# Value projections of attention and retention packed into three blocks of 256 columns, in a two-stage fp32 network on one core

## The chip, the core and the metric

The kernel runs on one core of one Trainium2 chip, in one launch. The metric is the device time of that core in microseconds (us), taken as the median of several executions. Engines are named as in the profile: PE is TensorE (PEld its weight loads), ACT is ScalarE, DVE is VectorE, POOL is GpSimd, SP is SyncE, which issues the DMAs.

## The reference

The input is one sequence of 512 tokens with 1,024 features. The first stage has two layers; the second stage (feed-forward, state-space scan, dilated attention, cross-attention, feed-forward) is untouched by the change and is left out here. A layer of the first stage is:

```
h = rms_norm(x, g_mix_pre)
u = h @ w_in                                   # 1024 -> 3*384 + 512 + 4*384 = 3200 columns
aq, ak, av, cu, rq, rk, rv, rg = jnp.split(u, SPLITS, axis=-1)
y_att  = chunk_attention(aq, ak, av, rel_bias)  # 6 heads of 64, softmax
y_conv = conv_module(cu, ...)                   # 31 taps, layer norm, silu
y_ret  = retention(rq, rk, rv, rg)              # 6 heads of 64, rotary, decay, layer norm, gate
mix = jnp.concatenate([y_att, y_conv, y_ret], axis=-1) @ w_out
x = x + rms_norm(mix, g_mix_post)
...                                             # then the MLP with w_up, w_down
```

`av` and `rv`, 384 columns each, are the two value projections that the change is about.

## The kernel before, in words

**Products in three parts.** Weights and activations are fp32 and are split into a rounded part (`w_hi`, `h_hi`) and a rest (`w_lo`, `h_lo`). A product is three matmuls per 128-deep slice of the contraction: hi by hi, hi by lo, lo by hi. `product` (line 360) does one block: for each output tile, 8 slices of 3 matmuls.

**Blocks.** The weights are cut into blocks of at most 256 columns (`WCOLS`), in a list made by `layer_pieces` (line 135). A layer has 50 of them. The first 14, which form `w_in`, are in this order (numbered within the layer):

- 0, 1: the convolution's input; 2, 3, 4: attention's queries and keys
- 5 (256 columns), 6 (128 columns): attention's values `av`
- 7, 8, 9: retention's queries and keys `rqk`
- 10 (256), 11 (128): retention's values `rv`
- 12 (256), 13 (128): retention's gate `rg`

Block 14 is the first of `w_out`. A block is of one of two kinds. In a "feat" block the weights are stationary and the 512 tokens stream, so each matmul has 512 columns and the block one tile per 128 output columns. In a "tok" block, which the values are, 128 tokens are stationary and the block's weight columns stream, so each matmul has 256 or 128 columns and there are four tiles, one per 128 tokens: 4 x 8 x 3 = 96 matmuls whether the block is 256 or 128 wide. Two "tok" tiles share a PSUM bank.

**What travels with a block.** Three engines prepare block n+2 while TensorE works: SP loads it into `w_raw` (`load_block`), ACT rounds it (`round_block`, line 339) after its copies of block n out of PSUM, and DVE subtracts to get the rest (`rest_block`, line 350). TensorE waits for that rest before the block. ACT copies each finished tile out of PSUM (`evacuate`, `evacuate_one`).

**The order of the work** is written out by hand for each engine, for one layer at a time; semaphores tie the engines together. From block 8 (`SOFT_AT`) on, attention's softmax is interleaved. It has 24 steps (6 heads by 4 query tiles of 128, the keys growing from 128 to 512 within a head). In step i TensorE (`attend`, line 767) does the scores of i, transposes the probabilities of i-2 (`turn`), and multiplies those of i-3 by the values (`mix`); in steps 8, 10, ... 18 it also does one `swapped` matmul for retention's rotary embedding. DVE (`attend`, line 1192) adds the bias to the scores of i, takes the reciprocal of the sum of i-1, the maximum of i, scales i-1, and in those even steps does three rotary instructions. ACT (`softmax`, line 987) takes the exponential of i and copies the transposed i-2 out of PSUM. The scores and the rotary swaps take turns in a ring of two PSUM banks, so scores wait until DVE has read the one two places before.

Steps are put in "feat" blocks halfway through each tile and behind it, in "tok" blocks only behind each tile: `slots_of` (line 616) gives a "feat" block two steps per tile and a "tok" block one. That makes 4 steps each in blocks 8 to 12 and 2 in block 13, 22 in all; the rest follow among retention's scores. DVE and ACT do the preparation of block n+2 behind the steps of block n.

Beside blocks 1 to 6 DVE computes the convolution's 62 taps, 11 per block; TensorE waits for the last behind block 7 (`MEAN_AT`).

Of the kernel before, what the change touches and what calls it, by code (L numbers as in the profile page):

```python
# [22 lines left out]
P = 128  # L23
# [110 lines left out]

def layer_pieces():

    out = []
    a = ATT_W

    def feat(c0, c1):  # L140
        for c in range(c0, c1, WCOLS):
            out.append(Piece(0, c, min(WCOLS, c1 - c), KD, "feat", "w_in"))

    def tok(c0, c1):
        for c in range(c0, c1, WCOLS):
            out.append(Piece(0, c, min(WCOLS, c1 - c), KD, "tok", "w_in"))


    feat(3 * a, 3 * a + 2 * CONV_W)
    feat(0, 2 * a)  # L150
    tok(2 * a, 3 * a)
    r = 3 * a + 2 * CONV_W
    feat(r, r + 2 * RET_W)
    tok(r + 2 * RET_W, r + 3 * RET_W)
    feat(r + 3 * RET_W, r + 4 * RET_W)
    for c in range(0, DM, WCOLS):
        out.append(Piece(0, c, WCOLS, KD, "feat", "w_out"))
    for half in range(2):
        for j in range(8):
            out.append(Piece(0, half * 2048 + j * WCOLS, WCOLS, KD, "feat", "w_up"))  # L160
        for j in range(4):
            for kb in range(2):
                out.append(Piece(half * 2048 + kb * KB, j * WCOLS, WCOLS, KD, "feat", "w_down",
                                 group=("down", half, j)))
    return out
# [56 lines left out]
def build(nc, ins, outs):  # L222
# [5 lines left out]
    with ExitStack() as ctx:  # L228
# [32 lines left out]
        av = at("av", [P, TOKT, ATT_W], F32, FZ + 12)  # L261
        rv = at("rv", [P, TOKT, RET_W], F32, FZ + 18)
# [12 lines left out]
        ret_sq = at("ret_sq", [P, 3, SEQ], F32, FZ + 12)  # L275
# [16 lines left out]
        def sq_tile(m):  # L292
            return conv_sq[:, m - 3, :] if m < 5 else ret_sq[:, m - 5, :]
# [305 lines left out]
        N_IN = 14  # L599
        W_OUT = 14  # L600
        UP = [18, 34]
        DOWN = [26, 42]
# [13 lines left out]
        def slots_of(b):  # L616

            return 2 * b.tiles if b.kind == "feat" else b.tiles
# [93 lines left out]
        def layer_tensor(pe, lay):  # L712
# [43 lines left out]
            def mix(s):  # L756
# [5 lines left out]
                for j in range(q + 1):  # L762
                    mm = pe.matmul(o_ps[r, P * q:P * q + P], av[:, j, HD * h:HD * h + HD],  # L763
                                   probs_t[:, s % 2, P * j:P * j + P], start=j == 0, stop=j == q)
# [22 lines left out]
            for b in plan1[2:N_IN]:  # L787
                if b.i < SOFT_AT:
                    product(pe, b, h_hi, h_lo)
                elif b.kind == "feat":  # L790
# [6 lines left out]
                else:  # L797
                    product(pe, b, h_hi, h_lo, between=lambda m: attend(slot0[b.i] + m))
# [16 lines left out]
            def ret_mixed(s):  # L815
# [5 lines left out]
                pe.matmul(ret_bank[h // 2][r, P * j:SEQ], rv[:, j, HD * h:HD * h + HD], ret_sc(h, j),  # L821
# [8 lines left out]
            def pair_var(j):  # L830
                pe.wait_ge(S["ln_sq_s"], cnt("ln_sq_s", 2 + j))
                for q in range(TOKT):
                    mm = pe.matmul(t_ps[:, 2 * q:2 * q + 2], ret_sq[:, j - 1, P * q:P * q + P],
                                   head_ones[:, 0:P:HD], start=True, stop=True)
# [78 lines left out]
        def layer_gpsimd(pool, lay):  # L913
# [20 lines left out]
            for b in plan1[12:14]:  # L934
                by_root(b, [rg[:, 2 * (b.i - 12) + m, :] for m in range(b.tiles)])
# [11 lines left out]
        def layer_scalar(act, lay):  # L947
# [64 lines left out]
            for b in plan1[2:N_IN]:  # L1012
                if b.i < 5:
                    evacuate(b, lambda m: qk[:, 2 * (b.i - 2) + m, :])
                elif b.i < 7:
                    evacuate(b, lambda m: av[:, m, 256 * (b.i - 5):256 * (b.i - 5) + b.w])
                elif b.i < SOFT_AT:
                    evacuate(b, lambda m: rqk[:, 2 * (b.i - 7) + m, :])
                elif b.kind == "feat":
                    dst, t = (rqk, 2 * (b.i - 7)) if b.i < 10 else (rg, 2 * (b.i - 12))  # L1020
# [6 lines left out]
                else:  # L1027
                    cols = slice(256 * (b.i - 10), 256 * (b.i - 10) + b.w)
                    for m in range(b.tiles):
                        if m % 2:  # L1030
                            for q in (m - 1, m):
                                evacuate_one(b, q, rv[:, q, cols])
                        softmax(slot0[b.i] + m)
# [1543 lines left out]
def laid_out(a):  # L2577
# [3 lines left out]
    layers = [packed(plan, ("w_in", a["w_in"][l]), ("w_out", a["w_out"][l]), ("w_up", a["w_up"][l]),  # L2581
# [46 lines left out]
```

## Time and profile before

| | us |
|---|---|
| median of 3 runs | 2773.67 |
| lowest, highest | 2772.21, 2774.31 |
| the profiled execution's own time | 2773.67 |
| its span in the profile | 2771.8 |

| engine | busy us | share of the span |
|---|---|---|
| PE | 2669.7 | 96% |
| PEld | 2109.0 | 76% |
| DVE | 1342.1 | 48% |
| ACT | 944.5 | 34% |
| POOL | 428.3 | 15% |

How to read it: the profile is of one execution. Matmuls are pipelined and the profile's duration of one includes its way through the array, so neighbouring matmuls overlap and what one costs in a stream is the distance from start to start, not its duration. Idle time of an engine that nothing waits for costs nothing. Layer 0's `w_in` blocks lie between 17 and 216 us of the span, layer 1's between 700 and 894 us.

### The profile page before, as it was taken

The numbers are of one execution on the slowest core, as the hardware profiler recorded it, in microseconds if no ns is written. First come the engines' busy times: TensorE is split into PE (matmuls) and PEld (weight loads), VectorE is DVE, ScalarE is ACT, GpSimd is POOL, SyncE is SP. The second block draws the span as 40 slices with busy tenths as digits, with TensorE's granted clock in tenths as the row PEclk, the third lists the DMA queues.
The fourth block names the chain that finished last, engine by engine and source line by source line (L and its number), as shares of the span: only waits on it lengthen the run. The fifth ranks groups of instructions, "written<-read, shape, count | busy, mean of one in ns | idle before, by whom it ended". The sixth has DMA issues, their size and how long they took to land.

```text
span 2771.8 us, 31517 instructions
## 1 busy us (share of the span) xinstructions
PE 2669.7 (96%) x12280; PEld 2109.0 (76%) x12280; DVE 1342.1 (48%) x1670; ACT 944.5 (34%) x1331; POOL 428.3 (15%) x375
## 2 busy tenths in 40 slices
PE   8999999999999999999899999999999997999998
PEld 6875788887877678888788888878776676788886
DVE  6744452333864454143443332597874456343422
ACT  4333442322333443232332232442335453322221
POOL 2101100001210110000211101176630320111100
PEclk9999999999999999999999999999999999999999
DMA  3310122232220112322122222411131023222222
GB/s 139 133 39 31 61 102 95 91 106 92 72 111 31 47 64 102 106 91 94 74 91 100 92 99 103 150 70 51 69 126 65 16 104 140 76 105 92 84 96 78
DMA packets 41003, 241.78 MB, mean 87 GB/s; under 512 B 4800, under 2 KB 5312, under 8 KB 17984
## 3 DMA queue, kind: packets, MB, share of 16 engines
q1 hardware_dynamic: 40624, 239.24, 24.3%
q8 instruction: 75, 1.23, 0.2%
q0 software_dynamic: 272, 1.05, 0.1%
q14 instruction: 32, 0.26, 0.0%
HBM read 231.88 MB, written 8.39 MB: 87 GB/s over the span
## 4 chain that ended last, share of the span: by engine, by line
PE 87%; DVE 7%; ACT 4%; issue 2%; DMA 0%; ACTq 0%; DVEq 0%; SPq 0%
PE gemm L388 71%; ACT w_hi L348 2%; DVE x_sb L534 2%; PE score L742 1%; PE mixed L763 1%; DVE w_lo L357 1%; PE gemm L572 1%; DVE h_lo L522 1%; PE mixed L1601 1%; ACT h_hi L517 1%; PE gemm L574 1%; PE score L1590 1%; PE gemm L573 1%; PE turned L753 1%; PE mixed L437 1%
## 5 line engine op out<-in xcount | busy, mean ns | idle before, releaser
L357 DVE TENSOR_TENSOR w_lo<-w_raw,w_hi 128x2048 fp32r<-128x2048 f32 (+3 forms) x225 | 473.2, 2103 | 651.0 <-ACT w_hi L348 650.7
L388 PE MATMUL gemm<-h_hi,w_hi 128*128 128x512 f32 x1744 | 692.8, 397 | 2.7 <-DVE w_lo L357 1.9
L388 PE MATMUL gemm<-h_hi,w_lo 128*128 128x512 f32 x1744 | 679.9, 390 | 0.0
L388 PE MATMUL gemm<-h_lo,w_hi 128*128 128x512 f32 x1744 | 679.1, 389 | 0.0
L348 ACT ACTIVATE w_hi<-w_raw 128x2048 fp32r<-128x2048 f32 (+3 forms) x225 | 393.4, 1749 | 438.9 <-PE gemm L388 401.0
L388 PEld LDWEIGHTS gemm<-h_hi,w_hi 128*128 128x128 f32 x1744 | 327.6, 188 | 75.8 <-issue 6.1
L388 PEld LDWEIGHTS gemm<-h_hi,w_lo 128*128 128x128 f32 x1744 | 327.3, 188 | 69.2
L388 PEld LDWEIGHTS gemm<-h_lo,w_hi 128*128 128x128 f32 x1744 | 327.8, 188 | 66.1 <-issue 1.7
L388 PE MATMUL gemm<-f_hi,w_hi 128*128 128x512 f32 x512 | 199.2, 389 | 0.0
L388 PE MATMUL gemm<-f_lo,w_hi 128*128 128x512 f32 x512 | 199.2, 389 | 0.0
L388 PE MATMUL gemm<-f_hi,w_lo 128*128 128x512 f32 x512 | 199.2, 389 | 0.0
L454 POOL TENSOR_TENSOR sq_f<-sq_f 128x512 f32<-128x512 f32 x30 | 47.7, 1590 | 750.6 <-ACT sq_f L432 653.1
L388 PE MATMUL gemm<-g_hi,w_hi 128*128 128x512 f32 x352 | 137.3, 390 | 0.0
L388 PE MATMUL gemm<-g_lo,w_hi 128*128 128x512 f32 x352 | 137.0, 389 | 0.0
L388 PE MATMUL gemm<-g_hi,w_lo 128*128 128x512 f32 x352 | 136.9, 389 | 0.0
L1749 POOL TENSOR_TENSOR swi<-swi,rs 128x512 f32<-128x512 f32 x44 | 56.9, 1295 | 411.3 <-ACT swi L1857 411.3
L572 PE MATMUL gemm<-h_hi,w_hi 128*128 128x512 f32 x192 | 85.7, 446 | 33.9 <-DVE h_lo L522 17.6
L388 PEld LDWEIGHTS gemm<-f_hi,w_hi 128*128 128x128 f32 x512 | 96.1, 188 | 20.1
L388 PEld LDWEIGHTS gemm<-f_hi,w_lo 128*128 128x128 f32 x512 | 96.1, 188 | 20.0
L388 PEld LDWEIGHTS gemm<-f_lo,w_hi 128*128 128x128 f32 x512 | 96.1, 188 | 19.8
L388 PE MATMUL gemm<-w_hi,h_hi 128*128 128x256 f32 (+1 forms) x352 | 107.6, 306 | 0.0
L388 PE MATMUL gemm<-w_lo,h_hi 128*128 128x256 f32 (+1 forms) x352 | 106.0, 301 | 0.0
(386 smaller groups left out, 3899.1 us busy)
## 6 DMA issues: line engine op xcount, KB each, us to landing
w_raw<-in_w SPq DMA_DIRECT2D x171, 1024.0 KB, 4.8
w_raw<-in_w SPq DMA_DIRECT2D x16, 768.0 KB, 4.0
w_raw<-in_w SPq DMA_DIRECT2D x16, 640.0 KB, 3.8
w_raw<-in_w SPq DMA_DIRECT2D x18, 512.0 KB, 3.6
bias_t<-in_att_bias SPq DMA_DIRECT2D x2, 1536.0 KB, 9.4
decay_t<-in_c_decay SPq DMA_DIRECT2D x2, 1536.0 KB, 8.0
x_sb<-in_x SPq DMA_DIRECT2D x4, 512.0 KB, 6.1
x_kept<-x_sb SPq DMA_DIRECT2D x1, 2048.0 KB, 10.9
```

The lines of the kernel that those rows point to most:

```text
L348: act.activation(w_hi[:, b.slot, 0:size], w_raw[:, b.slot, 0:size], ACT.Copy).then_inc(S["w_rounded"], 1)
L357: dve.tensor_tensor(w_lo[:, b.slot, 0:size], w_raw[:, b.slot, 0:size], w_hi[:, b.slot, 0:size].bitcast(F32), ALU.subtract).then_inc(S["w_r ...
L388: mm = pe.matmul(dst, lhs, rhs, start=b.first and k == 0 and j == 0, stop=b.last and k == b.kt - 1 and j == 2)
L437: mm = pe.matmul(o_ps[:, 0:n], ones[:], sq[:, k, :], start=k == 0, stop=k == KD - 1)
L454: pool.tensor_tensor(sq[:, 0, :], sq[:, 0, :], sq[:, k, :], ALU.add).then_inc(S["sq_added"], 1)
L517: act.activation(h_hi[:, k, :], x_sb[:, k, :], ACT.Copy, scale=gain[:, k:k + 1]).then_inc(S["norm_hi"], 1)
L522: dve.scalar_tensor_tensor(out=h_lo[:, k, :], in0=x_sb[:, k, :], scalar=gain[:, k:k + 1], in1=h_hi[:, k, :].bitcast(F32), op0=ALU.mult, op ...
L534: dve.tensor_tensor(x_sb[:, k, :], x_sb[:, k, :], out_sb[:, k, :], ALU.add).then_inc(S["x_done"], 1)
L572: pe.matmul(dst, wh[:, k, c], h_hi[:, k, :], start=k == 0, stop=False)
L573: pe.matmul(dst, wh[:, k, c], h_lo[:, k, :], start=False, stop=False)
L574: mm = pe.matmul(dst, wl[:, k, c], h_hi[:, k, :], start=False, stop=k == KD - 1)
L1749: pool.tensor_tensor(swi[:, m, :], swi[:, m, :], rs[:], ALU.mult).then_inc(S["silu_r"], 1)
```

## The change

The columns of `w_in` are put in another order on the host (`in_columns`), and the constants `QK_AT` and so on name the places in it. The two value projections lie side by side as 768 columns and are cut into three blocks of 256: block 5 holds the first 256 of `av`, block 6 the last 128 of `av` and the first 128 of `rv`, and block 10 the last 256 of `rv`. The gate becomes blocks 11 and 12, and `w_out` begins at block 13. A layer has 49 blocks, so that every later block's number falls by one (by two in the second stage). The values live in one tile `values`, which `value(c, j)` cuts. One of three small squares tiles moves to another place in memory (`ret_sq_last`).

`slots_of` gives a "tok" block two steps per tile as well, and `attend` is called halfway through its tiles too. Steps per block are now 4 in block 8, 4 in block 9, 8 in block 10, 4 in block 11 and 2 in block 12: again 22, with the same numbers doing the rotary work.

The diff (with context cut, and lines left out marked "..."):

```diff
@@ -132,6 +132,21 @@
...
+QK_AT = 2 * CONV_W
+VALUES_AT = QK_AT + 2 * ATT_W
+RQK_AT = VALUES_AT + ATT_W + RET_W
+RG_AT = RQK_AT + 2 * RET_W
+def in_columns(w):
+    a, r = ATT_W, 3 * ATT_W + 2 * CONV_W
+    parts = ((3 * a, r), (0, 2 * a), (2 * a, 3 * a), (r + 2 * RET_W, r + 3 * RET_W), (r, r + 2 * RET_W),
+             (r + 3 * RET_W, r + 4 * RET_W))
+    return np.concatenate([w[:, c0:c1] for c0, c1 in parts], axis=1)
 def layer_pieces():
@@ -146,13 +161,12 @@
...
-    feat(3 * a, 3 * a + 2 * CONV_W)
-    feat(0, 2 * a)
-    tok(2 * a, 3 * a)
-    r = 3 * a + 2 * CONV_W
-    feat(r, r + 2 * RET_W)
-    tok(r + 2 * RET_W, r + 3 * RET_W)
-    feat(r + 3 * RET_W, r + 4 * RET_W)
+    feat(0, 2 * CONV_W)
+    feat(QK_AT, QK_AT + 2 * a)
+    tok(VALUES_AT, VALUES_AT + 2 * WCOLS)
+    feat(RQK_AT, RQK_AT + 2 * RET_W)
+    tok(VALUES_AT + 2 * WCOLS, VALUES_AT + 3 * WCOLS)
+    feat(RG_AT, RG_AT + RET_W)
     for c in range(0, DM, WCOLS):
@@ -258,8 +272,11 @@
...
         qk = at("qk", [P, 6, SEQ], F32, FZ)
-        av = at("av", [P, TOKT, ATT_W], F32, FZ + 12)
-        rv = at("rv", [P, TOKT, RET_W], F32, FZ + 18)
+        values = at("values", [P, 3, TOKT, WCOLS], F32, FZ + 12)
+        def value(c, j):
+            return values[:, c // WCOLS, j, c % WCOLS:c % WCOLS + HD]
         rg = at("rg", [P, 3, SEQ], F32, FZ + 24)
@@ -272,7 +289,8 @@
...
         conv_sq = at("conv_sq", [P, 2, SEQ], F32, FZ + 46.25)
-        ret_sq = at("ret_sq", [P, 3, SEQ], F32, FZ + 12)
+        ret_sq = at("ret_sq", [P, 2, SEQ], F32, FZ + 12)
+        ret_sq_last = at("ret_sq_last", [P, SEQ], F32, FZ + 60.5)
@@ -290,7 +308,7 @@
...
         def sq_tile(m):
-            return conv_sq[:, m - 3, :] if m < 5 else ret_sq[:, m - 5, :]
+            return conv_sq[:, m - 3, :] if m < 5 else ret_sq[:, m - 5, :] if m < 7 else ret_sq_last[:]
@@ -596,10 +614,10 @@
...
-        N_IN = 14
-        W_OUT = 14
-        UP = [18, 34]
-        DOWN = [26, 42]
+        N_IN = 13
+        W_OUT = 13
+        UP = [17, 33]
+        DOWN = [25, 41]
         PAIRS = RET_HEADS // 2
@@ -615,7 +633,7 @@
...
-            return 2 * b.tiles if b.kind == "feat" else b.tiles
+            return 2 * b.tiles
@@ -760,7 +778,7 @@
...
                 for j in range(q + 1):
-                    mm = pe.matmul(o_ps[r, P * q:P * q + P], av[:, j, HD * h:HD * h + HD],
+                    mm = pe.matmul(o_ps[r, P * q:P * q + P], value(HD * h, j),
                                    probs_t[:, s % 2, P * j:P * j + P], start=j == 0, stop=j == q)
@@ -787,15 +805,13 @@
...
                     product(pe, b, h_hi, h_lo)
-                elif b.kind == "feat":
+                else:
                     def after(m):
...
                     product(pe, b, h_hi, h_lo, halfway=lambda m: attend(slot0[b.i] + 2 * m), between=after)
-                else:
-                    product(pe, b, h_hi, h_lo, between=lambda m: attend(slot0[b.i] + m))
                 if b.i == MEAN_AT:
@@ -818,7 +834,7 @@
...
                 r = slice(HD * (h % 2), HD * (h % 2) + HD)
-                pe.matmul(ret_bank[h // 2][r, P * j:SEQ], rv[:, j, HD * h:HD * h + HD], ret_sc(h, j),
+                pe.matmul(ret_bank[h // 2][r, P * j:SEQ], value(ATT_W + HD * h, j), ret_sc(h, j),
                           start=j == 0, stop=j == TOKT - 1).then_inc(S["ret_mix"], 1)
@@ -830,7 +846,7 @@
...
                 for q in range(TOKT):
-                    mm = pe.matmul(t_ps[:, 2 * q:2 * q + 2], ret_sq[:, j - 1, P * q:P * q + P],
+                    mm = pe.matmul(t_ps[:, 2 * q:2 * q + 2], sq_tile(4 + j)[:, P * q:P * q + P],
                                    head_ones[:, 0:P:HD], start=True, stop=True)
@@ -931,8 +947,8 @@
...
             by_root(plan1[9], [rqk[:, 4 + m, :] for m in range(2)])
-            for b in plan1[12:14]:
-                by_root(b, [rg[:, 2 * (b.i - 12) + m, :] for m in range(b.tiles)])
+            for b in plan1[11:13]:
+                by_root(b, [rg[:, 2 * (b.i - 11) + m, :] for m in range(b.tiles)])
             pool.wait_ge(S["ln_done"], cnt("ln_done", 2))
@@ -1013,11 +1029,11 @@
...
                 elif b.i < 7:
-                    evacuate(b, lambda m: av[:, m, 256 * (b.i - 5):256 * (b.i - 5) + b.w])
+                    evacuate(b, lambda m: values[:, b.i - 5, m, :])
                 elif b.i < SOFT_AT:
...
                 elif b.kind == "feat":
-                    dst, t = (rqk, 2 * (b.i - 7)) if b.i < 10 else (rg, 2 * (b.i - 12))
+                    dst, t = (rqk, 2 * (b.i - 7)) if b.i < 10 else (rg, 2 * (b.i - 11))
                     for m in range(b.tiles):
@@ -1025,12 +1041,12 @@
...
                 else:
-                    cols = slice(256 * (b.i - 10), 256 * (b.i - 10) + b.w)
                     for m in range(b.tiles):
+                        softmax(slot0[b.i] + 2 * m)
                         if m % 2:
                             for q in (m - 1, m):
-                                evacuate_one(b, q, rv[:, q, cols])
-                        softmax(slot0[b.i] + m)
+                                evacuate_one(b, q, values[:, 2, q, :])
+                        softmax(slot0[b.i] + 2 * m + 1)
                 if b.i + 2 < W_OUT:
@@ -2578,7 +2594,7 @@
...
     out["x"] = np.ascontiguousarray(a["x"][0].T)
-    layers = [packed(plan, ("w_in", a["w_in"][l]), ("w_out", a["w_out"][l]), ("w_up", a["w_up"][l]),
+    layers = [packed(plan, ("w_in", in_columns(a["w_in"][l])), ("w_out", a["w_out"][l]), ("w_up", a["w_up"][l]),
                      ("w_down", a["w_down"][l])) for l in range(DEPTH)]
```

**The steps on TensorE, first half of block 10, layer 0.** `gemm` is the block's PSUM bank, `score`, `turned` and `mixed` the banks of scores, transposes and outputs. Before (steps 8 and 9; the "..." are seven more trios like the one above it):

```order
L742 MATMUL score<-qk 128x128
L734 MATMUL score<-rqk,swap_sb 128x512
L753 MATMUL turned<-ident_sb,probs 128x128 x3
L763 MATMUL mixed<-out_sb,av 64x128 x2
L388 MATMUL gemm<-w_hi,h_hi 128x256
L388 MATMUL gemm<-w_lo,h_hi 128x256
L388 MATMUL gemm<-w_hi,h_lo 128x256
...
L742 MATMUL score<-qk 128x256
L753 MATMUL turned<-ident_sb,probs 128x128 x4
L763 MATMUL mixed<-out_sb,av 64x128 x3
```

Now (the "..." are three more trios):

```order
L760 MATMUL score<-qk 128x128
L752 MATMUL score<-rqk,swap_sb 128x512
L771 MATMUL turned<-ident_sb,probs 128x128 x3
L781 MATMUL mixed<-out_sb,values 64x128 x2
L406 MATMUL gemm<-w_hi,h_hi 128x256
L406 MATMUL gemm<-w_lo,h_hi 128x256
L406 MATMUL gemm<-w_hi,h_lo 128x256
...
L760 MATMUL score<-qk 128x256
L771 MATMUL turned<-ident_sb,probs 128x128 x4
L781 MATMUL mixed<-out_sb,values 64x128 x3
```

Between two steps of block 10 stood 24 matmuls of 256 columns, and 24 of 128 columns in block 11; now 12 of 256 columns stand there, and steps 8 to 15 are all in block 10.

**DVE, from the end of block 9's steps into step 8, layer 0.** Before:

```order
L1217 TENSOR_SCALAR probs<-probs,tiny 128x384
L357 TENSOR_TENSOR w_lo<-w_raw,w_hi 128x1024
L1203 SCALAR_TENSOR_TENSOR probs<-score,bias_t 128x128
L1208 RECIPROCAL tiny<-tiny 128x1
L1212 TENSOR_REDUCE tiny<-probs 128x1
L1217 TENSOR_SCALAR probs<-probs,tiny 128x512
L1160 TENSOR_TENSOR rot_a<-rqk,cos_t 128x512
```

Now:

```order
L1233 TENSOR_SCALAR probs<-probs,tiny 128x384
L375 TENSOR_TENSOR w_lo<-w_raw,w_hi 128x2048
L1219 SCALAR_TENSOR_TENSOR probs<-score,bias_t 128x128
L1224 RECIPROCAL tiny<-tiny 128x1
L1228 TENSOR_REDUCE tiny<-probs 128x1
L1233 TENSOR_SCALAR probs<-probs,tiny 128x512
L1176 TENSOR_TENSOR rot_a<-rqk,cos_t 128x512
```

The order is the same, but block 11 is now 256 wide, and so its rest (`w_lo`), which stands ahead of step 8, has twice the elements. The next rest, of block 12, now stands ahead of step 16 with 1,024 elements per partition; before it stood ahead of step 12 with 2,048.

**ACT, step 10 to step 11, layer 0.** `probs` is the exponential, `turned` the transposed copy, `rv` or `values` two tiles of the block. Before:

```order
L992 ACTIVATE probs,tiny<-probs,tiny 128x384
L1001 ACTIVATE out_sb<-turned 128x128
L1006 ACTIVATE out_sb<-mixed 128x512
L985 ACTIVATE rv<-gemm,tiny 128x256 x2
L992 ACTIVATE probs,tiny<-probs,tiny 128x512
L1001 ACTIVATE out_sb<-turned 128x256
L348 ACTIVATE w_hi<-w_raw 128x2048
```

Now:

```order
L1008 ACTIVATE probs,tiny<-probs,tiny 128x384
L1017 ACTIVATE out_sb<-turned 128x128
L1022 ACTIVATE out_sb<-mixed 128x512
L1001 ACTIVATE values<-gemm,tiny 128x256 x2
L1008 ACTIVATE probs,tiny<-probs,tiny 128x512
L1017 ACTIVATE out_sb<-turned 128x256
```

The block's tiles are copied out in pairs between two steps, twice in block 10 as before; the rounding that followed step 11 has gone from there.

## Rows read from the trace of the kernel before

**Rows 1.** The page, part 4: chain that ended last, shares of the span by engine

```profile
PE 87%; DVE 7%; ACT 4%; issue 2%; DMA 0%; ACTq 0%; DVEq 0%; SPq 0%
```

**Rows 2.** Timeline, TensorE: starts of blocks 5, 6, 7 in layer 0; of 5 and 7 in layer 1

```profile
74.54 0.28 PE L388 MATMUL gemm<-w_hi,h_hi 128*128 128x256 f32 x1
...
86.05 0.22 PE L388 MATMUL gemm<-w_hi,h_hi 128*128 128x128 f32 x1
...
96.72 0.44 PE L388 MATMUL gemm<-h_hi,w_hi 128*128 128x512 f32 x1
...
752.28 0.28 PE L388 MATMUL gemm<-w_hi,h_hi 128*128 128x256 f32 x1
...
774.46 0.44 PE L388 MATMUL gemm<-h_hi,w_hi 128*128 128x512 f32 x1
```

**Rows 3.** Timeline, TensorE, layer 0: starts of blocks 10, 11, 12

```profile
145.83 0.39 PE L388 MATMUL gemm<-w_hi,h_hi 128*128 128x256 f32 x1
...
167.26 0.33 PE L388 MATMUL gemm<-w_hi,h_hi 128*128 128x128 f32 x1
...
187.76 0.50 PE L388 MATMUL gemm<-h_hi,w_hi 128*128 128x512 f32 x1
```

**Rows 4.** Timeline, TensorE, layer 0: starts of steps 8, 9, 11; the first transposes of step 8

```profile
148.88 0.48 PE L742 MATMUL score<-qk 64*128 64x128 f32 x2
...
150.26 0.49 PE L753 MATMUL turned<-ident_sb,probs 128*128 128x128 f32 x3
...
154.33 0.70 PE L742 MATMUL score<-qk 64*128 64x256 f32 x2
...
165.48 1.12 PE L742 MATMUL score<-qk 64*128 64x512 f32 x2
```

**Rows 5.** Timeline, VectorE, layer 0: rests ahead of steps 8 and 12; step 8

```profile
148.72 1.23 DVE L357 TENSOR_TENSOR w_lo<-w_raw,w_hi 128x1024 fp32r<-128x1024 f32 x1 [1.77 <-ACT w_hi L348]
149.86 0.28 DVE L1203 SCALAR_TENSOR_TENSOR probs<-score,bias_t 128x128 f32<-128x128 f32 x1
...
150.38 0.48 DVE L1217 TENSOR_SCALAR probs<-probs,tiny 128x512 f32<-128x512 f32 x1
...
152.17 0.69 DVE L1164 TENSOR_TENSOR rqk<-rot_a 128x512 f32<-128x512 f32 x1
...
171.01 2.29 DVE L357 TENSOR_TENSOR w_lo<-w_raw,w_hi 128x2048 fp32r<-128x2048 f32 x1 [2.63 <-ACT w_hi L348]
```

**Rows 6.** Timeline, ScalarE, layer 0: rounding; the copy of step 8

```profile
147.64 1.05 ACT L348 ACTIVATE w_hi<-w_raw 128x1024 fp32r<-128x1024 f32 x1
...
150.90 0.47 ACT L1001 ACTIVATE out_sb<-turned 128x384 f32<-128x384 f32 x1
...
169.07 1.90 ACT L348 ACTIVATE w_hi<-w_raw 128x2048 fp32r<-128x2048 f32 x1
```

**Rows 7.** Timeline, TensorE, layer 0: end of attention; what it waited for in brackets

```profile
221.30 1.02 PE L742 MATMUL score<-qk 64*128 64x512 f32 x2
...
225.03 0.52 PE L753 MATMUL turned<-ident_sb,probs 128*128 128x128 f32 x3 [1.98 <-ACT out_sb L1001]
```

**Rows 8.** Timeline, ScalarE, VectorE, TensorE: the last taps beside block 7

```profile
96.92 0.63 ACT L964 ACTIVATE av<-gemm,tiny 128x128 f32<-128x128 f32 x2 [4.73 <-PE gemm L388]
97.44 1.92 ACT L348 ACTIVATE w_hi<-w_raw 128x2048 fp32r<-128x2048 f32 x1
...
154.44 0.84 ACT L985 ACTIVATE rv<-gemm,tiny 128x256 f32<-128x256 f32 x2 [3.06 <-PE gemm L388]
...
101.60 5.76 DVE L1149 SCALAR_TENSOR_TENSOR out_sb<-ca,par_sb,out_sb 128x512 f32<-128x512 f32 x7
...
107.70 1.88 PE L719 MATMUL turned<-out_sb,ones_sb 128*128 128x512 f32 x4
```

**Rows 9.** Stretches: us, busy PE, PEld, DVE, ACT, POOL, granted clock, DMA share, GB/s

```profile
226.00:240.00 14.00, 14.00 (x70) 5.75 (x68) 4.50 (x10) 7.15 (x12) 0.00 (x0) 0.88 0.01 2
257.00:264.00 7.00, 7.00 (x27) 5.50 (x29) 4.06 (x5) 2.55 (x3) 0.00 (x0) 0.55 0.35 142
```

## The prediction

> **What bounds the kernel now.** I read the chain of waits by engine first: TensorE holds 87% of it [rows 1]. So the place of the change is read as TensorE's time, and for the other engines I ask only whether they are late for it. Next the timeline of TensorE over the value projections, because their matmuls overlap there and only the distance between starts tells their cost. Undisturbed by attention, layer 0's block 5 (96 matmuls of 256 columns) runs from 74.54 to 86.05 us, and block 6 (96 of 128 columns) from 86.05 to 96.72 [rows 2]. That is 11.51 and 10.67 us, or 120 and 111 ns a matmul: half the columns save 7%. Layer 1's pair takes 22.18 us against 22.18 [rows 2]. Blocks 10 and 11, with four attention steps each, take 21.43 and 20.50 us [rows 3]; less 11.51 and 10.67 this leaves 9.92 and 9.83 us for the steps, 19.75 for eight. TensorE does not wait in any of these steps in the timeline, so DVE and ACT are ahead of it there, with a margin that has to be measured. The last steps of attention show what happens without one: the transposes wait 1.98 us for ACT [rows 7].
>
> **The change, part by part (per layer).**
>
> Block 6 grows from 128 to 256 columns: 11.51 - 10.67 = 0.84 us more on TensorE [rows 2].
>
> Blocks 10 and 11 become one. 21.43 + 20.50 = 41.93 us becomes 11.51 + 19.75 = 31.26, 10.67 us less [rows 3]. The net is 10.67 - 0.84 = 9.83 us, and 19.66 us in two layers. It lies on TensorE's path in full. Here the row speaks against a rule: the Trainium skill, "TensorE: Matmul & The Clock Gate", section "Wait — 56ns, not 53.3ns?", gives back-to-back matmuls at full clock N / 2.4 GHz plus about 2.5 ns from start to start. By it 192 matmuls of 128 columns (55.8 ns) take 10.7 us, 96 of 256 columns (109.2 ns) 10.5 us, and the sum would be an estimated 0.5 us for both layers instead of 19.66. The trace disagrees at 128 columns with 111 ns; I take the trace.
>
> Work off TensorE: one rounding, one rest and eight copies out of PSUM fewer, and one DMA fewer with the same bytes in all. I cost them at nothing, since TensorE did not wait for any of them. Two of them get longer or move, and these are checked in turn.
>
> *The taps beside block 7.* ACT's rounding of block 8 begins at 97.44 us, 0.72 behind the end of block 6 [rows 2, 8]. Block 6 now ends 0.84 later, and the pair of copies ahead of the rounding takes 0.84 us at 256 columns where the narrow pair took 0.63 [rows 8]. So DVE's rest and its last seven taps move by about 1.05 us, from an end of 101.60 + 5.76 = 107.36 to 108.41. TensorE comes for them at 107.70 [rows 8], now at 108.54. The cover shrinks from 0.34 to 0.13 us: no wait, at most 0.2 a layer.
>
> *The rest ahead of step 8.* Block 11 is now 256 wide, so ACT's rounding takes 1.90 us instead of 1.05 from 147.64 [rows 6], and DVE's rest begins 0.85 later, at 149.57. The narrow rest holds DVE for 149.86 - 148.72 = 1.14 us of its 1.23; the wide one, 2.29, then holds it for 2.20 [rows 5]. Step 8's bias add begins on DVE at 151.77. Counting on with the rows' own distances: the scaling of step 7 begins 0.52 later and ends at 152.77 [rows 5], and ACT's copy, 1.04 behind the bias add and 0.47 long, ends at 153.28 [rows 5, 6]. TensorE's step 9 needs both. And TensorE now comes sooner: block 10 starts at 145.83 [rows 3], its first 24 matmuls took 3.05 us [rows 4], the first 12 take 3.05 - 1.44 = 1.61 (a half tile is 11.51 / 8 = 1.44), so step 8 starts at 147.44. Step 8's own work is 154.33 - 148.88 - 2.88 = 2.57 us [rows 4], and step 9 starts at 147.44 + 2.57 + 1.44 = 151.45. Its transposes would follow its scores, some 0.6 us on (the scores' row of 0.70 less the overlap), at 152.05. They can start at about 153.35: **a new wait of 1.3 us.** (Its scores wait too, for DVE to read the bank of step 8, at 152.05; that is inside the same 1.3.) Bounds: zero if ACT reaches the rounding earlier, since nothing else holds it; above, the 1.98 us of rows 7. I take 1.3, since each term has its own row.
>
> *The other steps.* A step of block 10 came every 5.4 us (step 8); now it comes every 2.57 + 1.44 = 4.0. DVE needs 149.86 to 152.17 + 0.69 = 3.00 us for it with its rotary part [rows 5], so it stays 1 us ahead, and the delay of step 8 is absorbed. The longest way round is a step with 512 keys: from scores through DVE, ACT's exponential and ACT's copy to the next transposes 225.03 - 221.30 = 3.73 us [rows 7]. Step 11 gives it its own work, 167.26 - 165.48 = 1.78 [rows 3, 4], half a tile of 1.44, and the scores and swap of step 12, 1.38 as in step 8 [rows 4]: 4.60 us. The margin is 0.9 us, and ACT's pair of copies (0.84) falls into the time in which DVE works. No wait. Block 12's rest now stands ahead of step 16, but there half a tile is 2.7 us (12 matmuls of 512 columns) and the rest a narrow one. From block 11 on, the order is that of block 12 before. The moved squares tile and the new PSUM bank order in layer 0 change no wait that I can find.
>
> **Sum.** 2773.67 (the profiled execution, which equals the median of the runs) - 19.66 + 2 x 1.3 = **2756.6 us**.
>
> **The rivals.** A measurement of this kernel can tell about 0.2%, 5.5 us.
>
> A. *The clock falls behind the new wait.* The granted clock was 0.88 over 226 to 240 us, just behind the wait of 1.98 us, and 0.55 over 257 to 264, behind several short ones [rows 7, 9]. A stretch like the second costs 7 x 0.45 = 3.2 us a layer. Then 2759.8 (one layer) to 2763.0 (both). For: block 10 is now full of small interruptions with one wait in it. Against: one wait of 1.3 us is shorter than either cause. The reverse, that layer 0's dip (14 x 0.12 = 1.7 us) goes away, gives 2754.9; without the new wait as well, 2752.3.
>
> B. *DVE and ACT can't hold the pace of 4 us.* The margins of 0.9 and 1.0 us are gone and the four rotary steps each wait a further microsecond: 8 us, 2764.6. For: the delay of step 8 meets a rotary part at once. Against: the three margins above.
>
> C. *The narrow matmuls cost nothing extra.* If the merged block took as long as the two it replaces (the same columns in all), nothing would be saved, and only the wait is left: 2773.67 + 2.6 = 2776.3. The rule of the Trainium skill above would bring it to about this place. Against it stand the two neighbours in rows 2, the plainest rows here.
>
> D. *Slower: every step in block 10 waits as the last steps of attention do.* Eight steps a layer at 1.98 us are 31.7 us, against 19.66: 2785.7. It decides from 19.66 / 16 = 1.23 us per step. For: rows 7 show that closely packed steps do wait. There, though, only small matmuls stand between them.
>
> **How the numbers follow.** Forecast 0.67, its own range 2754 to 2759. A 0.13, B 0.11, C 0.03, D 0.02, and 0.04 for what I have not seen, half of it still faster. Faster by over 0.2% means below 2768.1: the forecast, A, B and 0.02, together 0.93. Within: 0.01 of the rest and 0.02 of C, 0.03. Slower: 0.04. The range takes in the wait's bounds and A on both sides, 2752.3 to 2763.0; B lies above it.
>
> **What would show it.** Right: blocks 5 and 6 each 11.5 us in both layers; block 10, with eight steps, 31 to 33 us; one wait of about 1.3 us on TensorE in step 9 for ACT's copy or DVE's read; blocks behind it as before. Wrong: waits in steps 10 to 15 (B, D), a granted clock under 1.00 between blocks 10 and 12 (A), a merged block of 256 columns longer than 12 us net of its steps (C), or a wait for the taps behind block 7.

## The result and the profile after

| | before | after |
|---|---|---|
| median of 5 runs each, us | 2773.89 | 2759.49 |
| lowest, highest | 2772.21, 2774.54 | 2757.43, 2762.52 |
| the profiled execution's own time | 2773.67 | 2757.58 |

The ratio is 0.9948 with a 95% interval of 0.9937 to 0.9959: 14.4 us less. The prediction was 2756.6, 17.1 us less, in a range of 2752.3 to 2763.0. A second round of five runs of the same kernel gave 2759.9 (2758.24 to 2762.09), 0.994 [0.9926, 0.9953].

The page of after, the engines' busy time and the chain by engine. It answers to [rows 1]:

```profile
PE 2650.2 (96%) x12088; PEld 2089.0 (76%) x12088; DVE 1338.8 (49%) x1668; ACT 942.7 (34%) x1321; POOL 427.8 (16%) x375
...
PE 86%; DVE 7%; ACT 4%; issue 2%; DMA 1%; ACTq 0%; DVEq 0%; SPq 0%
```

TensorE bounds the kernel as before, with 19.5 us less busy time and 192 matmuls fewer, 96 in each layer.

TensorE's timeline in layer 0 of after: the starts of blocks 5 and 7, the layer norm behind block 7, then block 10 with step 8, the two waits of step 9, steps 10, 11 and 13, the start of block 11 (the end of block 10), and step 16:

```profile
74.77 0.28 PE L406 MATMUL gemm<-w_hi,h_hi 128*128 128x256 f32 x1
...
97.81 0.40 PE L406 MATMUL gemm<-h_hi,w_hi 128*128 128x512 f32 x1
...
108.71 0.68 PE L737 MATMUL turned<-out_sb,ones_sb 128*128 128x512 f32 x1
...
146.91 0.39 PE L406 MATMUL gemm<-w_hi,h_hi 128*128 128x256 f32 x1
...
148.52 0.48 PE L760 MATMUL score<-qk 64*128 64x128 f32 x2
...
153.19 0.70 PE L760 MATMUL score<-qk 64*128 64x256 f32 x2 [0.60 <-DVE probs L1219]
154.51 0.63 PE L771 MATMUL turned<-ident_sb,probs 128*128 128x128 f32 x4 [0.62 <-ACT out_sb L1017]
...
157.49 0.91 PE L760 MATMUL score<-qk 64*128 64x384 f32 x2
...
162.13 0.69 PE L760 MATMUL score<-qk 64*128 64x512 f32 x1
...
169.53 0.70 PE L760 MATMUL score<-qk 64*128 64x256 f32 x2
...
179.58 0.50 PE L406 MATMUL gemm<-h_hi,w_hi 128*128 128x512 f32 x1
...
182.55 0.48 PE L760 MATMUL score<-qk 64*128 64x128 f32 x2
```

Blocks 5 and 6 take 97.81 - 74.77 = 23.04 us where they took 22.18 [rows 2]. Block 10 takes 179.58 - 146.91 = 32.67 us where blocks 10 and 11 took 41.93 [rows 3], 9.26 less. From step 16 (190.73 before) the distance between the two kernels stays at 8.18 us to the end of attention. Layer 1 repeats both differences and both waits, within 0.02 us.

The cause of the waits, in the timelines of VectorE and ScalarE of after: the rest of block 11 and the bias add of step 8; the rounding, and ScalarE's copy of step 8. They answer to [rows 5, 6]:

```profile
150.65 2.29 DVE L375 TENSOR_TENSOR w_lo<-w_raw,w_hi 128x2048 fp32r<-128x2048 f32 x1 [2.62 <-ACT w_hi L366]
152.86 0.28 DVE L1219 SCALAR_TENSOR_TENSOR probs<-score,bias_t 128x128 f32<-128x128 f32 x1
...
148.72 1.90 ACT L366 ACTIVATE w_hi<-w_raw 128x2048 fp32r<-128x2048 f32 x1
...
153.89 0.47 ACT L1017 ACTIVATE out_sb<-turned 128x384 f32<-128x384 f32 x1
```

Everything lies 1.08 us later than in the prediction's count, because blocks 5 and 6 are longer and block 5 begins 0.23 later; the distances are the predicted ones: rounding to rest 1.93, rest to bias add 2.21, bias add to the end of the copy 1.50 (1.51 was counted).

The taps behind block 7, in VectorE's timeline (they answer to [rows 8]): they end at 108.64, and TensorE comes at 108.71 and does not wait.

```profile
102.89 5.75 DVE L1165 SCALAR_TENSOR_TENSOR out_sb<-ca,par_sb,out_sb 128x512 f32<-128x512 f32 x7
```

The clock, in stretches of after that answer to [rows 9] (columns: stretch, its length, busy PE, PEld, DVE, ACT, POOL, granted clock, DMA share, GB/s):

```profile
140.00:183.00 43.00, 41.78 (x225) 28.54 (x224) 23.89 (x54) 15.52 (x38) 1.41 (x2) 1.00 0.07 25
...
226.00:240.00 14.00, 12.31 (x70) 5.61 (x70) 8.01 (x17) 10.53 (x17) 1.56 (x1) 1.00 0.01 2
880.00:890.00 10.00, 8.02 (x33) 3.46 (x34) 4.58 (x11) 2.59 (x8) 0.00 (x0) 0.83 0.00 1
```

The granted clock is given as a share of TensorE's higher level: 1.00 is 2.4 GHz, 0.50 the lower level, 1.2 GHz, and a value between is read here as a stretch that has both. It did not fall in block 10. Layer 0's dip behind attention (0.88 before) is gone, and layer 1 has one (0.83) that it did not have before. Over the whole span, adding 1 minus the granted clock over stretches of 10 us and up to 2740 us, the clock cost 41.0 us of full speed before and 40.9 after. So the profiled executions compare cleanly: 2773.67 - 2 x 9.26 + 2 x 0.86 = 2756.9, and 2757.58 was measured.

### The profile page after: what moved, and what is told of

It is laid out like the page before. It is cut to its first block, busy times and chain, and to the rows that moved or that the text cites. A ratio compares the mean times of both kernels' runs of the same rounds, so it can differ in the third digit from the quotient of the medians.

```text
span 2755.8 us, 31122 instructions
## 1 busy us (share of the span) xinstructions
PE 2650.2 (96%) x12088; PEld 2089.0 (76%) x12088; DVE 1338.8 (49%) x1668; ACT 942.7 (34%) x1321; POOL 427.8 (16%) x375
## 4 chain that ended last, share of the span: by engine, by line
PE 86%; DVE 7%; ACT 4%; issue 2%; DMA 1%; ACTq 0%; DVEq 0%; SPq 0%
PE gemm L406 71%; ACT w_hi L366 2%; DVE x_sb L552 2%; PE score L760 1%; DVE w_lo L375 1%; PE mixed L781 1%; PE gemm L590 1%; DVE h_lo L540 1%; PE mixed L1617 1%; ACT h_hi L535 1%; PE gemm L592 1%; PE gemm L591 1%; PE score L1606 1%; PE mixed L455 1%; PE score L1661 1%
## 5 line engine op out<-in xcount | busy, mean ns | idle before, releaser
L1101 ACT ACTIVATE tt<-tt 128x512 f32<-128x512 f32 x64 | 40.3, 632 | 190.8 <-DVE tt L1317 190.8
L1317 DVE SCALAR_TENSOR_TENSOR tt<-gemm,rs 128x512 f32<-128x512 f32 x64 | 43.7, 687 | 103.3 <-PE gemm L406 101.8
```

The costliest lines, as they stand in the source:

```text
L1101: act.activation(tt[:, 2 * j + m, :], tt[:, 2 * j + m, :], ACT.Square).then_inc(S["f_sq"], 1)
L1317: dve.scalar_tensor_tensor(out=tt[:, 2 * j + m, :], in0=tile_of(b, m), scalar=0.0, in1=rs[:], op0=ALU.max, op1=ALU.mult).then_inc(S["g_fre ...
```

## The experiments

**1. The same kernel again.** It answers whether the distance of the median to the profiled execution is the kernel's or the run's.

> The changed kernel once more, unaltered, beside the others of this call. My theory: TensorE loses 9.83 us a layer of value projection and gains one wait of 1.2 us a layer, in step 9; median about 2759, and the profile shows the same two waits (0.60 and 0.62 us) in each layer. The five runs lay between 2757.4 and 2762.5 us with granted clocks of 0.983 to 0.981: if that spread is the clock's (rival A), the runs with the lower mean clock are again the longer ones, some 2.5 us per 0.001; if it is something else, time and clock do not go together.

Measured: 2759.9. By granted clock its five runs are 2758.24 and 2759.15 (0.983), 2759.9 and 2760.89 (0.982) and 2762.09 (0.981). The kernel before, 15 times on that chip, does the same: 2772.4 to 2772.8 at 0.984, 2773.7 to 2774.8 at 0.983, 2776.3 to 2777.8 at 0.982. The profiled execution took 2760.89, 3.3 more than the first one of this kernel. Both have the same two waits in step 9. In two stretches the clock falls in the second profile and not in the first. Here they are, first in the first profile, then in this one:

```profile
2050.00:2060.00 10.00, 9.23 (x50) 7.71 (x51) 4.54 (x18) 5.51 (x18) 0.00 (x0) 1.00 0.28 115
2070.00:2080.00 10.00, 7.37 (x43) 6.02 (x42) 6.12 (x17) 4.65 (x14) 0.00 (x0) 1.00 0.36 122
```

```profile
2050.00:2060.00 10.00, 9.14 (x43) 7.50 (x44) 3.89 (x15) 4.67 (x16) 0.00 (x0) 0.83 0.23 95
2070.00:2080.00 10.00, 7.37 (x33) 5.85 (x32) 4.12 (x9) 4.45 (x11) 0.00 (x0) 0.83 0.37 131
```

Two times 10 x 0.17 is 3.4 us, the whole difference, at a place that the change does not touch. (The other dips are in both, some a little displaced; over the whole span the second profile loses 44.6 us, the first 40.9.) Block 5 begins at 74.63 us here and at 74.77 in the first profile, so that 0.14 of difference comes from the execution alone. What follows: executions of one kernel differ by some 5 us (2757.4 to 2762.5, and 2772.4 to 2777.8 before), the longer ones at the lower clock. From here runs are compared at equal clock, or by the timeline. At 0.983 the change is worth about 15.6 us on this chip, at 0.982 about 16.5.

**2. The steps packed, the widths as before.** The kernel before, with eight steps in block 10 and none in block 11:

```diff
-            return 2 * b.tiles
+            if b.kind == "feat":
+                return 2 * b.tiles
+            return 8 if b.i == 10 else 0
...
-                elif b.kind == "feat":
+                elif b.kind == "feat" or b.i == 10:
...
-                    product(pe, b, h_hi, h_lo, between=lambda m: attend(slot0[b.i] + m))
+                    product(pe, b, h_hi, h_lo)
```

ScalarE's order is changed to match.

> The kernel before, with its four value blocks, but steps 8 to 15 all in block 10 (256 wide, two per tile) and none in block 11 (128 wide). This is the second half of the change alone. My theory: the density costs nothing, since the wait needs the wide rest of block 11, and that is narrow here; by the rows the copy ends at 151.4 and step 9 needs it at 152.0. So the time is that of the kernel before, 2773.7, within 1.5 us, with no wait in steps 8 to 15. Rivals B and D: dense steps wait by themselves, 2776 (one wait a layer) to 2805 (all of them).

Measured: 2774.45 (2772.67 to 2776.28), ratio 0.9995 [0.9986, 1.0004]. TensorE's timeline, steps 9 and 13:

```profile
151.55 0.70 PE L744 MATMUL score<-qk 64*128 64x256 f32 x2
...
167.22 0.70 PE L744 MATMUL score<-qk 64*128 64x256 f32 x2
```

A step comes every 3.4 to 4.6 us, as in the changed kernel, and no step from 8 to 15 waits. From step 7 to step 16 it takes 46.82 us (144.15 to 190.97), against 46.69 before. What follows: packing neither costs nor gains by itself. So the gain is in the widths, and the wait needs the wide rest, which experiments 3 and 4 test.

**3. The rest of block 11 done twice.** The changed kernel, VectorE doing the suspected instruction a second time, with the same result:

```diff
-                if b.i + 2 < W_OUT:
+                if b.i == 9:
+                    again = plan[b.n + 2]
...
+                    for _ in range(2):
...
+                        dve.tensor_tensor(w_lo[:, again.slot, 0:WSIZE], w_raw[:, again.slot, 0:WSIZE],
+                                          w_hi[:, again.slot, 0:WSIZE].bitcast(F32), ALU.subtract).then_inc(
+                            S["w_rest" if _ else "again"], 1)
+                elif b.i + 2 < W_OUT:
```

> The changed kernel, with DVE's rest of block 11 done twice in a row (the same values). This lengthens the suspected cause by 2.2 us and a semaphore's round, some 2.3 us, in each layer. My theory: what stands ahead of step 8's bias add is passed on one for one, since TensorE waits for it already: the waits in step 9 grow from 1.2 to 3.5 us a layer, 4.6 us in all, about 2764. If the wait's cause is elsewhere: no change. If the longer wait also brings the clock down: 2 to 6 us more than 2764.

Measured: 2766.0 (2763.91 to 2768.6), ratio 0.9964 [0.995, 0.9977]: 6.1 us above the changed kernel on the same chip. VectorE's and TensorE's timelines, then the granted clock behind the wait:

```profile
150.45 4.62 DVE L1252 TENSOR_TENSOR w_lo<-w_raw,w_hi 128x2048 fp32r<-128x2048 f32 x2 [2.62 <-ACT w_hi L366]
154.98 0.28 DVE L1219 SCALAR_TENSOR_TENSOR probs<-score,bias_t 128x128 f32<-128x128 f32 x1
...
155.32 1.04 PE L760 MATMUL score<-qk 64*128 64x256 f32 x2 [2.92 <-DVE probs L1219]
156.64 1.09 PE L771 MATMUL turned<-ident_sb,probs 128*128 128x128 f32 x4 [0.28 <-ACT out_sb L1017]
...
155.00:165.00 10.00, 9.40 (x37) 6.55 (x37) 5.75 (x17) 2.67 (x9) 0.00 (x0) 0.66 0.30 107
```

The second rest (2.33 us more on VectorE) makes the waits 3.20 us instead of 1.22, 1.98 more a layer, 4.0 in both; that leaves 2.1 of the 6.1 us, which I put down to the clock. (The two profiles on this chip fit only roughly: the clock cost 45.9 us of full speed here and 44.6 in experiment 1, 1.3 more.) What follows: step 8's bias add does stand behind that rest, and nearly all of the added time arrives at TensorE. And right behind a wait of this size the clock falls, to 0.66 over ten microseconds, 3.4 us of full speed; behind 1.22 it stayed at 1.00 in both layers of both profiles. In layer 1 it is 0.76 over 830 to 840 us and 0.83 over 820 to 840. So the mechanism of rival A exists in this kernel and costs what it was priced at (3.2 us a layer), but the change's own wait did not set it off. Other dips of the span are absent here, which is why the whole costs only 1.3 us more.

**4. The rounding earlier.** ScalarE rounds block 11 ahead of the softmax of step 7 instead of behind it:

```diff
+                        if b.i == 9 and m == b.tiles - 1:
+                            round_block(act, b.n + 2)
...
-                if b.i + 2 < W_OUT:
+                if b.i + 2 < W_OUT and b.i != 9:
```

> ACT rounds block 11 between its copy of block 9's last tile and the exponential of step 7, not behind step 7. My theory: the wait in step 9 comes from rounding plus rest standing ahead of step 8's bias add. The rounding fits in an idle time of 1.9 us, so DVE's rest begins about 2.6 us earlier and both waits of step 9 are gone: 2 x 1.2 = 2.4 us less than the changed kernel, about 2757. Rival B (eight steps in 11.5 us are too dense in themselves, the first rotary part above all): the wait stays or moves to a later step, no change of time.

Measured: 2755.66 (2751.69 to 2756.01), ratio 0.9922 [0.9909, 0.9936]. Timelines of VectorE and TensorE, the rest, the bias add and step 9:

```profile
147.72 2.29 DVE L375 TENSOR_TENSOR w_lo<-w_raw,w_hi 128x2048 fp32r<-128x2048 f32 x1
149.92 0.28 DVE L1221 SCALAR_TENSOR_TENSOR probs<-score,bias_t 128x128 f32<-128x128 f32 x1
...
152.31 0.70 PE L760 MATMUL score<-qk 64*128 64x256 f32 x2
152.93 0.66 PE L771 MATMUL turned<-ident_sb,probs 128*128 128x128 f32 x4
```

Both waits are gone, in both layers. The median fell by 4.2 us; 2.4 of it are the waits, and the rest goes with the clock (0.983 to 0.985 here, 0.981 to 0.983 in experiment 1). At 0.983 the means lie 2.8 us apart. What follows: the wait that the change brought is one of order, not of work, and an edit of three lines takes it back.

The same kernel on another chip, beside experiment 9:

> The changed kernel with ScalarE's rounding of token block 11 ahead of the normalisation of step 7, once more, beside the kernel with the filled tail. Theory: 2752 to 2756 as at first, at a granted clock of 0.983 to 0.985, so that runs at the same clock lie 2 to 3.5 us under those of the changed kernel (2757.4 to 2759.2 at 0.983), which is both waits of step 9 in two layers. Rival (the first result was its chip's clock): 2757 to 2760 here.

Measured: 2756.5 (2752.49 to 2758.58), ratio 0.9929 [0.9915, 0.9942], with no wait in step 9. At 0.984 its runs took 2752.49 and 2753.64, at 0.983 2756.5 and 2756.53, at 0.982 2758.58; the changed kernel's four runs at 0.983 took 2757.4 to 2759.2. The median is 0.5 us above the span that was expected, and at equal clock the kernel is 0.9 to 2.7 us shorter, less than the 2 to 3.5 expected: the clock, given to three places, leaves about 2 us open. The waits in the timeline are the firmer proof.

**5 to 8. What a narrow matmul costs.** Four kernels in which the "tok" blocks of `w_in` use fewer columns, or fewer stationary tokens, at the same number of matmuls, so that a part of the values is not computed. The edit of the first; the others put 64 for the columns, or for the tokens (and for the partitions of `dst`):

```diff
+                        cols = slice(0, b.w)
+                        if b.src == "w_in":
+                            cols = slice(0, 128)
+                            dst = bank[b.bank + m // 2][0:128, (m % 2) * 256:(m % 2) * 256 + 128]
+                            h, r = hi[:, k, m * P:m * P + 128], lo[:, k, m * P:m * P + 128]
```

128 tokens, 128 columns:

> The changed kernel, with only the first 128 of the 256 columns computed in each matmul of the three value blocks (half of the values are left out); the number of matmuls stays at 96 a block. My theory: 111 against 120 ns from start to start, 10.67 against 11.51 us a block, six blocks: 5.0 us less, less 0.4 us that the wait in step 9 grows; about 2755. The rule that TensorE's time goes by columns: 128 columns at 2.4 GHz are 53 ns, times 576 matmuls, 30.7 us less: about 2729.

128 tokens, 64 columns:

> As cols128, but only 64 of the 256 columns (three quarters of the values are left out). Theory: below some 240 columns the weight load sets the distance, 111 ns however few columns stream: blocks of 10.6 to 10.7 us, the same time as cols128. Rival: a fixed part plus a part by columns; from 120 ns at 256 and 111 at 128 a straight line gives 107 at 64, blocks of 10.3 us.

64 tokens, 64 columns:

> As cols64, and only 64 of each tile's 128 tokens are loaded as stationary operand (seven eighths of the values are left out). This halves the weight load. Theory (the load of the stationary operand is the floor of 111 ns): the distance falls to about 56 to 65 ns, blocks of 5.4 to 6.3 us. Rival (the floor is a fixed cost of issuing a pair of load and matmul): it stays near 111 ns.

64 tokens, 256 columns:

> All 256 columns, but only 64 of each tile's 128 tokens as stationary operand (half of the values are left out). Theory: at 256 columns the streaming, 107 ns, has just overtaken the load, so a shorter load changes the distance of 120 ns by little: 110 to 120 ns. If the load still were the floor at 256 columns, it would fall well below 107.

Measured in TensorE's timeline, from the first of the 192 matmuls of blocks 5 and 6 to the first of block 7, or, with 64 columns, between matmuls ahead of the point where the clock falls:

| stationary tokens | columns | from start to start at full clock, ns | median of the kernel, us |
|---|---|---|---|
| 128 | 256 (the changed kernel) | 120 | 2759.49 |
| 128 | 128 | 111 | 2760.28 (10 runs) |
| 128 | 64 | 112 | 2801.15 (1 run) |
| 64 | 256 | 113 | 2753.56 (1 run) |
| 64 | 64 | 58 | 2756.64 (1 run) |

The ends of the row with 128 columns, (96.08 - 74.69) / 192 = 111 ns:

```profile
74.69 0.22 PE L411 MATMUL gemm<-w_hi,h_hi 128*128 128x128 f32 x1
...
96.08 0.45 PE L411 MATMUL gemm<-h_hi,w_hi 128*128 128x512 f32 x1
```

With 128 tokens and 64 columns, 36 distances in 4.02 us:

```profile
74.77 0.28 PE L411 MATMUL gemm<-w_hi,h_hi 128*128 128x64 f32 x1
...
78.79 0.30 PE L411 MATMUL gemm<-w_hi,h_hi 128*128 128x64 f32 x1
```

With 64 tokens and 64 columns, ten distances in 0.58 us:

```profile
75.19 0.22 PE L411 MATMUL gemm<-w_lo,h_hi 128*64 128x64 f32 x1
...
75.77 0.22 PE L411 MATMUL gemm<-w_hi,h_lo 128*64 128x64 f32 x1
```

From 128 columns to 64 nothing is saved (111 and 112 ns; a straight line through 120 and 111 had given 107); halving the stationary operand halves the distance (112 to 58). So the price of a narrow matmul here is the load of its stationary operand, and each of these matmuls has a load of its own. That is the floor on which the 128-wide blocks of the kernel before lay: 111 ns for half the columns that 120 ns carry. The Trainium skill, "TensorE: Matmul & The Clock Gate", section "LDWEIGHTS (loading the stationary operand)", gives a load as the operand's columns over 1.2 in ns, 107 for 128 and 53 for 64. The trace agrees to within 5 ns, with 111 to 112 and 58. The column rule of the Trainium skill that the prediction weighs (same page, section "Wait — 56ns, not 53.3ns?") gives 55.8 ns for 128 columns. The trace has 111, so the rule does not hold for these matmuls. The section "Back-to-back issue gap" of the same page of the Trainium skill has about 81 ns for streams of load and matmul at 128 columns. The trace disagrees with that too. No run here has another type of data, so whether the type makes the difference stays open.

The kernel with 128 columns was expected near 2755. At a clock of 0.983 its runs were there (2753.8 to 2754.0); the others went up to 2774.2 at 0.975. Its profile (2765.84, 0.978) shows where the clock was lost: not in blocks 5 and 6, where it is 1.00 in both layers, but in block 10, behind the waits of step 9 (0.86 and 0.62 us in layer 0). Layer 0 and layer 1 (columns as above):

```profile
152.00:162.00 10.00, 9.38 (x29) 5.91 (x29) 4.69 (x13) 2.50 (x9) 0.00 (x0) 0.52 0.31 107
...
820.00:840.00 20.00, 18.72 (x61) 12.05 (x61) 9.80 (x23) 4.68 (x13) 0.00 (x0) 0.54 0.15 53
```

There a wait and narrow matmuls come together. With 256 columns and 64 tokens waits of nearly that length (0.79 and 0.62 us) were followed by 0.83 in layer 0, and by 1.00 in layer 1:

```profile
152.00:162.00 10.00, 9.38 (x49) 6.77 (x48) 6.61 (x16) 3.43 (x10) 0.00 (x0) 0.83 0.29 107
```

So at 128 columns the share of the narrow matmuls in the fall is not shown. The kernel with 64 columns shows them alone. Its stretches at the start and in the middle of blocks 5 and 6, then behind them (columns as above):

```profile
74.00:80.00 6.00, 6.00 (x49) 5.88 (x48) 6.00 (x9) 2.40 (x2) 1.28 (x1) 0.91 0.21 85
80.00:111.00 31.00, 31.00 (x147) 31.00 (x147) 18.94 (x24) 4.31 (x7) 0.00 (x0) 0.50 0.32 119
112.00:130.00 18.00, 18.00 (x67) 13.70 (x66) 10.62 (x10) 5.18 (x6) 2.77 (x2) 0.88 0.38 146
```

TensorE is busy and its loads follow each other without a gap, and yet the clock stands at half speed for the 31 us; the distance from start to start is 213 ns there. Layer 1 does the same, 0.50 over 772 to 801 us, and in neither layer does TensorE wait in these blocks. The clock comes back while block 7 runs, with 512 columns a matmul. With 64 columns this costs more than the whole change gained. With 64 tokens and 64 columns the distance doubles too, from 58 to 107 ns, but there it is behind a wait of 1.91 us for the rest of block 6. What follows: rival C falls by direct measurement, and matmuls of 64 columns cost twice, by their floor and by the clock. The kernel before did not pay the second price for its narrow blocks: in its profile the clock is 1.00 over 74 to 97 and 145 to 188 us, and over the same blocks of layer 1.

**9. The tail filled.** Experiment 4's kernel, with two of retention's score steps ahead of the last attention step, where TensorE waits 1.98 us [rows 7]:

```diff
+            two(ret_scores, 2)
             attend(N_SLOT + 2)
-            two(ret_scores, 2)
```

> This is the changed kernel with two edits: ScalarE rounds token block 11 ahead of the normalisation of step 7, and two of the retention's score steps are issued ahead of the last attention step instead of behind it, so that TensorE has work while that last step waits for its copy on ScalarE (1.98 us in the trace of before, [rows 7]). Theory (TensorE sets the end there too, a wait filled with work that is due anyway is won whole, but two score steps are only some 1 us of work): 0.8 to 1.7 us less in each layer than with the first edit alone, at the same granted clock 1.7 to 3.4 us less in all, 2751 to 2754. Rival (VectorE and ScalarE are what is late there, and the wait only moves to the next reader): same as with the first edit alone, 2752 to 2756. Rival on the clock: with the wait gone the clock falls elsewhere, the time goes by the clock of the run alone, and runs at 0.983 are not shorter than 2755.

Measured: 2751.99 (2750.62 to 2753.39), ratio 0.9918 [0.9904, 0.9931]. TensorE's timeline at the end of attention in layer 0, and the clock of layer 1 over the same work; below, both of the kernel with the early rounding alone:

```profile
215.53 0.52 PE L771 MATMUL turned<-ident_sb,probs 128*128 128x128 f32 x3 [1.01 <-ACT out_sb L1017]
...
880.00:890.00 10.00, 10.00 (x62) 5.04 (x62) 4.90 (x11) 5.72 (x9) 0.00 (x0) 1.00 0.00 1
...
900.00:925.00 25.00, 21.87 (x104) 15.21 (x101) 13.31 (x19) 6.29 (x10) 4.53 (x2) 0.86 0.25 85
```

```profile
216.04 0.52 PE L771 MATMUL turned<-ident_sb,probs 128*128 128x128 f32 x3 [1.98 <-ACT out_sb L1017]
...
880.00:890.00 10.00, 8.02 (x41) 3.81 (x40) 5.07 (x12) 2.17 (x5) 0.00 (x0) 0.83 0.00 1
...
900.00:925.00 25.00, 21.55 (x116) 13.63 (x115) 15.76 (x23) 9.58 (x14) 4.60 (x3) 0.93 0.24 85
```

The wait is 0.97 us shorter, in both layers, since the two steps of 1.0 us in all now stand in it; from step 9 to `w_out` layer 0 takes 93.93 us instead of 94.90. In layer 1 the dip of 1.7 us behind the wait is gone as well, but over 900 to 925 us the clock then loses 3.5 us of full speed where it lost 1.8, so that nothing is gained by it. At 0.984 the runs are 2750.6 to 2752.0 against 2752.5 and 2753.6 for experiment 4's kernel, 1.8 less by their means, which is the two waits' 1.9 and the low end of what was expected. At 0.983 the means lie 3.3 apart, its high end. The rest of the 4.5 us between the medians goes with the clock. This is the fastest version, 2774.01 - 2751.99 = 22.0 us below the kernel before on its chip.

## Why the prediction was right

- **The merged blocks.** 10.67 us less were counted for block 10, and 1.3 back for the wait, 9.37 in all; 9.26 came. Step by step: the steps' own work and the half tiles came as counted, as experiment 2 shows for the steps alone.
- **Block 6.** 0.84 counted, 0.86 measured.
- **The new wait.** 1.3 us were counted at step 9, for the bias add behind the wide rest and ScalarE's copy; 0.60 + 0.62 = 1.22 came, at the scores first and then at the transposes, both by that chain. The prediction took both to be inside one interval, and they are. Experiment 3 lengthened it by its cause and experiment 4 removed it by its cause.
- **The margins behind it.** The 0.9 and 1.0 us for steps 10 to 15 held: no wait there, so B and D fall. Experiment 2, with the same pace, has none either.
- **The taps.** 0.13 us of cover were counted, 0.07 were left (108.64 against 108.71). It held, by less than the prediction's own rounding could promise.
- **The sum.** 2756.6 against 2757.58 for the profiled execution. Of the 1.0 us, 0.3 are the terms above (2756.9), 0.23 a later start of block 5 before anything that the change touches; the last 0.5 were not traced. The median, 2759.49, lies 0.5 above the forecast's own 2754 to 2759, and inside the whole range of 2752.3 to 2763.0.
- **Rival A.** It was put at 0.13 as a fall behind the new wait. That did not happen. But the spread that it stood for is there: the median lies 2.9 us above the forecast, and the runs with more of it have a lower clock (2757.4 at 0.983 to 2762.5 at 0.981). The prediction treated the clock as a matter of the change; experiment 1 shows that it moves the time by some 5 us from run to run with no change at all, before and after. The range was wide enough for this, for another reason than the one it gave, so that it held the median is in part luck. How near the new wait came to setting off a fall is not shown either: 1.22 us did not, 1.41 us did in one layer of experiment 8's kernel, and 3.20 us did in both of experiment 3's.
- **Rival C.** Refuted by experiments 5 to 8 in the distance itself, which the timelines had shown before the change.

## What to carry to other kernels

Read what a matmul costs from start to start in a stream. Where each matmul loads its own stationary operand, as here, a load of 128 columns sets a floor (111 to 112 ns), and a block of 128 moving columns costs 93% of one of 256. Blocks of a ragged width are worth joining, even across two consumers.

When two blocks are joined, ask which engine prepares the wider one, and what stands behind that preparation in its order: here one 2.2 us instruction on an engine that is half idle made TensorE wait, and moving another engine's instruction up by one step undid it. Filling a wait with work that is due anyway won that work's time and no more (0.97 us a layer): the dip behind the wait went, and a later stretch lost as much.

## What was not expected of the hardware

- With 64 columns against a stationary operand of 128 the clock fell although TensorE was never idle: 0.50 over 31 us, with TensorE and its loads busy throughout, in both layers of one execution. At 128 columns it stayed at 1.00 in blocks 5 and 6 of the one profile and fell behind the waits of block 10; the times of that kernel spread most (2753.8 to 2774.2).
- A wait of 3.2 us in a stream of 256-column matmuls was followed by 0.66 over ten microseconds, waits of 1.22 us by nothing, waits of 1.41 us by 0.83 in one layer and by nothing in the other; the wait of 1.98 us at the end of attention by 0.83 in layer 1 of all four profiles of the changed kernel and experiment 4's, but in layer 0 of only one of them. What decides there stays open.
- Halving the stationary tokens at 256 columns still saves a little, 120 to 113 ns, although a load of 64 has a floor of only 58. So at 256 columns the distance still depends a little on the load; what part each has was not separated.
